# Four value pages per interruption instead of two in the decode attention of a hybrid layer, on one Trainium2 core

## What is computed

```python
xn = rms_norm(x, g_mix)
z = jnp.einsum('btd,dc->btc', xn, w_in)            # q | k | v | forget logits | lru x | lru gate
att = forgetting_attention(q, k_all, v_all, logf_all, n_past)   # 8 heads of 128
lru = jax.nn.gelu(gl) * hs                          # conv, gates, RG-LRU
x = x + jnp.einsum('btc,cd->btd', concat(rms_norm(att), rms_norm(lru)), w_out)
x = x + jnp.einsum('btf,fd->btd', square(relu(rms_norm(x) @ w_up)), w_down)
```

## Time and profile before

| | |
|---|---|
| median of 3 runs | 2301.18 us (2300.08 to 2302.46) |
| span of the profiled execution, first to last instruction | 2298.8 us |
| TensorE busy | 2255.5 us, 98% |
| granted TensorE clock, mean | 0.994 |
| VectorE busy | 1605.5 us, 70% |
| moved | 368.47 MB, mean 160 GB/s |
| step period in the loop | 67.2 us |

### The profile page before, as it was taken

How to read it: one execution, slowest core, us unless ns; L and a number is a source line. 1 busy time by engine, 2 the same in 40 slices (tenths; PEclk the granted TensorE clock), 3 DMA queues, 4 the chain that set the end, 5 groups by cost and what they waited for, 6 DMA issues and landing times.

```text
span 2298.8 us, 50026 instructions
## 1 busy us (share of the span) xinstructions
PE 2255.5 (98%) x19889; PEld 2196.1 (96%) x19889; DVE 1605.5 (70%) x2043; ACT 858.9 (37%) x1201; POOL 154.0 (7%) x194
## 2 busy tenths in 40 slices
PE   7999999999999999999999999999999999999997
PEld 6999898989988999999999999999999999999997
DVE  7349889988884597876576576576576576576563
ACT  5124433344454233343243243243243243243245
POOL 0001111111114031000000000000000000000002
PEclk8999999999999999999999999999999999999998
DMA  7458999999985333333433433433433433433422
GB/s 239 106 159 261 323 330 327 317 314 327 317 290 191 98 127 84 114 96 99 138 93 98 137 93 98 137 93 99 137 94 98 137 93 99 137 93 99 137 89 97
DMA packets 386972, 368.47 MB, mean 160 GB/s; under 512 B 12259, under 2 KB 350596, under 8 KB 385844
## 3 DMA queue, kind: packets, MB, share of 16 engines
q1 hardware_dynamic: 359828, 295.38, 41.9%
q0 software_dynamic: 18608, 67.64, 8.2%
q10 hardware_dynamic: 8448, 4.20, 0.6%
HBM read 354.22 MB, written 12.94 MB: 160 GB/s over the span
## 4 chain that ended last, share of the span: by engine, by line
PE 87%; DVE 6%; DVEq 2%; issue 2%; ACT 1%; DMA 1%; SPq 1%; ACTq 0%
PE PS L1896 37%; PE PS L1900 18%; PE PS L2344 9%; PE PS L2343 9%; PE PS L2342 9%; DVE KR L1349 2%; PE PS L2057 2%; DVEq L1507 1%; PE PS L2105 1%; DVE WL L1213 1%; PE PS L2247 1%; DVE SC L1351 0%; ACT WH L743 0%; PE PS L2095 0%; DVE NM L1506 0%
## 5 line engine op out<-in xcount | busy, mean ns | idle before, releaser
L1093 ACT ACTIVATE WH<-RAW 128x1024 fp32r<-128x1024 f32 x293 | 304.9, 1056 | 679.8 <-PE PS L1900 521.5
L1647 DVE TENSOR_TENSOR WL<-RAW,WH 128x1024 fp32r<-128x1024 f32 x293 | 358.3, 1223 | 133.8 <-ACT WH L1093 132.4
L1896 PE MATMUL PS<-XH,WH 128*128 128x260 f32 x1952 | 408.6, 291 | 10.4 <-DVE XL L1278 6.2
L1896 PE MATMUL PS<-HH,WH 128*128 128x260 f32 x2048 | 412.5, 282 | 1.4 <-DVE HL L1652 0.7
L1900 PE MATMUL PS<-HH,WL 128*128 128x260 f32 x2048 | 411.7, 282 | 0.0
L1896 PE MATMUL PS<-HL,WH 128*128 128x260 f32 x2048 | 410.8, 282 | 0.0
L1896 PE MATMUL PS<-XL,WH 128*128 128x260 f32 x1952 | 393.7, 283 | 0.0
L1900 PE MATMUL PS<-XH,WL 128*128 128x260 f32 x1952 | 393.3, 283 | 0.0
L1750 DVE TENSOR_TENSOR A<-A,PS 128x520 f32<-128x520 f32 x256 | 177.5, 696 | 264.5 <-PE PS L1900 263.8
L1896 PEld LDWEIGHTS PS<-XH,WH 128*128 128x128 f32 x1952 | 301.4, 189 | 28.3 <-issue 19.5
L1896 PEld LDWEIGHTS PS<-HH,WH 128*128 128x128 f32 x2048 | 314.6, 188 | 2.1 <-issue 1.1
(11 more groups left out here) (335 smaller groups left out, 3085.6 us busy)
## 6 DMA issues: line engine op xcount, KB each, us to landing
KR<-in_cache_k POOLq DMA_DIRECT2D x128, 512.0 KB, 6.0
VR<-in_cache_v SPq DMA_DIRECT2D x128, 512.0 KB, 6.3
RAW<-in_w_up SPq DMA_DIRECT2D x128, 512.0 KB, 4.2
RAW<-in_w_down SPq DMA_DIRECT2D x128, 512.0 KB, 4.5
RAW<-in_w_in SPq DMA_DIRECT2D x82, 512.0 KB, 6.6
RAW<-in_w_out SPq DMA_DIRECT2D x32, 512.0 KB, 5.5
TMP<-in_w_up SPq DMA_DIRECT2D x30, 512.0 KB, 6.1
xT_spill<-A SPq DMA_DIRECT2D x1, 4160.0 KB, 16.3
```

The costliest lines, as they stand in the source:

```text
L1093: nc.scalar.activation(RING_H[SLOT[i]], RB[b], ACT.Copy).then_inc(f_hi, 1)
L1647: V.tensor_tensor(RING_L[SLOT[i]], RB[op_block(i)], RING_H[SLOT[i]].bitcast(F32), ALU.subtract).then_inc(f_lo, 1)
L1896: mm(dsts[c], wh(k), x[:, k, c * HT:(c + 1) * HT], start=first and n == 0 and x is xh, stop=False)
```

## The change

`values` takes a third argument, the number of pages. In the steps it is now four (NVS, the ring's size) instead of two, at the places (1, 21), (2, 21), (3, 21) for pages 0 to 3, 4 to 7, 8 to 11, and at (0, 21) of the next step for pages 12 to 15. The places (2, 5), (3, 5), (0, 5) and (1, 3) fall away. The interruption for pages 10 and 11 of sequence 6 in the first output unit falls away too, since step 7 now has them at (3, 21). All later calls keep two pages. SyncE's, GpSimd's, VectorE's and ScalarE's instructions are the same, in the same order.

```diff
-        VALUES_AT = {(1, 21): 0, (2, 5): 2, (2, 21): 4, (3, 5): 6, (3, 21): 8}
-        OLDER_AT = {(0, 5): 10, (0, 21): 12, (1, 3): 14}
+        VALUES_AT = {(1, 21): 0, (2, 21): 4, (3, 21): 8}
+        OLDER_AT = {(0, 21): 12}
...
-            def values(h, b0):
+            def values(h, b0, pages):
...
-                for b in (b0, b0 + 1):
+                for b in range(b0, b0 + pages):
                     pe.wait_ge(v_full[b % NVS], 16 * (NPG // NVS * h + b // NVS + 1))
...
-                        f.append(lambda: values(i - 1, VALUES_AT[q, n]))
+                        f.append(lambda: values(i - 1, VALUES_AT[q, n], NVS))
                     if prev and older and (q, n) in OLDER_AT:
-                        f.append(lambda: values(i - 2, OLDER_AT[q, n]))
+                        f.append(lambda: values(i - 2, OLDER_AT[q, n], NVS))
...
-                if k == NH + 1:
-                    values(last_b - 1, 10)
                 if k == NH + 4:
-                    values(last_b - 1, 12)
+                    values(last_b - 1, 12, 2)
```

More of the change, by code:

```diff
@@ L2273, in head_scores @@
                 value_cols(last_b - 1)
-            out_unit(1, {3: [lambda: values(last_b - 1, 14)], 7: [lambda: max_rows(NB, MT_LAST)], 11: [lambda: max_all(NB, MAX_LAST)],
+            out_unit(1, {3: [lambda: values(last_b - 1, 14, 2)], 7: [lambda: max_rows(NB, MT_LAST)], 11: [lambda: max_all(NB, MAX_LAST)],
                          14: [head_scores]})
[L2277 to L2281, removed]
+            out_unit(2, {7: [lambda: transpose_probs(h)], 13: [lambda: values(last_b, 0, 2)], 19: [lambda: attend(h)],
+                         27: [lambda: values(last_b, 2, 2)]})
+            out_unit(3, {3: [lambda: values(last_b, 4, 2)], 11: [lambda: values(last_b, 6, 2)], 19: [lambda: values(last_b, 8, 2)],
+                         27: [lambda: values(last_b, 10, 2)]})
+            out_unit(4, {3: [lambda: values(last_b, 12, 2)], 11: [lambda: values(last_b, 14, 2)], 17: [last_states], 23: [merge_sums]})
             out_unit(5, {5: [lambda: value_cols(last_b)], 13: [lru_sums]})
```

## The result

The change makes the kernel slower: 2344.41 us (median of 4 runs, 2336.95 to 2346.56) against 2300.63 (4 runs, 2298.89 to 2302.46), a ratio of 1.0184 with the interval [1.0172, 1.0196]. The profiled execution is the fastest of the four, 2336.95 us, with a span of 2335.3; all that follows accounts for its 36.5 us over the span before, and the other three runs are 6 to 10 us longer for a reason that no trace shows. Forecast were 2332 us with the range 2303 to 2348.

What follows compares the result with a forecast made beforehand. A step was taken as VectorE's piece (24.1 us) plus TensorE's piece (the other 43). Path +2.1 and page 11's waits 28.7 gave 30.8 us on the median 2301.2: 2332 us, range 2303 to 2348.

Steps and rivals of the forecast that it cites:

- main term: At (3, 21), page 11 lands later than the 14.9 us after page 8's request allowed; seven waits, 28.7 us.
- 6.5 and 7.1 for sequences 0 and 5: Page 11's forecast lateness at (3, 21), the two longest of seven; the others 2.5 to 3.8 us.
- The landing taken as fixed: Page 11's landing at (3, 21) does not move with earlier requests, which only queue; hence 28.7 us, not 8.
- A: The forecast case: waits for page 11 at (3, 21), full clock, 2325 to 2337 us; chance 0.60.
- C: Rival: earlier requests for pages 10 and 11 help, waits together 8 us, time 2311; chance 0.11.
- can now be requested some 3 us earlier: Pages 10 and 11: slots free after (2, 21), so SyncE need not wait for (3, 5).
- VectorE's piece, gain 0: From `max_all` to normalization, 24.1 us: 1.49 us less TensorE work becomes wait at the transposes, 0.44 to about 1.9.
- The wait for XL behind the gates: After step 7, first output unit: TensorE's 0.93 us wait becomes about 2, so the dropped interruption gains 0.
- The path's own +2.1: TensorE's work without new waits: +0.25 us in each of six passages, +1.5, and +0.56 after step 7.
- The shield at (0, 21): The wait at (3, 21) moves the need for pages 12 to 15 back by as much, so they hold.
- rival B: Clock falls in long waits: two falls of 3.9 us, 2340; in all seven, 2359; chance 0.13.
- the granted clock under 1.00 between 200 and 669 us: Sign of being wrong: this clock reading in the steps would point to B, the clock falling in long waits.

Runs made afterwards that it cites:

- wait-alone kernel: Kernel before, nothing merged; TensorE also waits at (3, 21) until pages 10 and 11 have landed; 2340.12 us, ratio 1.0171.
- experiment 4: The changed kernel, but in unit 3 SyncE requests pages 8 to 11 ahead of the weight unit; 2313.97 us, ratio 1.0052.
- Experiment 6: Kernel before with one pair merged: pages 0 to 3 at (1, 21), (2, 5) gone; 2299.51 us in one run.
- Experiment 5: The changed kernel with all four pages requested ahead of the weights in units 3 and 0, steps 1 to 7; 2304.51 us, ratio 1.0016.
- experiment 3: The changed kernel with 18 unread products added between pages 9 and 10 at (3, 21); 2331.18 us, ratio 1.0127.

## Why the prediction was right, and where not

- **The verdict and its main term.** "Page 11 is the fourth, and too late" was right in each of seven steps and is most of the loss; the sum was 28.7 us forecast, 24.8 measured, and 28.9 as idle time in the wait-alone kernel.
- **Which sequences.** Forecast were 6.5 and 7.1 for sequences 0 and 5; measured were 6.04, 5.87 for 0 and 1, and 3.01 for 5. Step by step the forecast took one trace for a pattern. (Its rows 7 leave out sequences 1 to 3; the trace has them, 18.7, 17.8 and 17.4 us from page 8's request to page 11's landing.) Where the weights stand between the pages, page 11 lands 20 to 22 us after page 8's request in at most two sequences of seven and 16.7 to 19.7 in the rest, and the long ones differ: 0 and 5 before, 0 and 1 after, 3 and 4 in the wait-alone kernel. Whether they move between runs of one kernel no second trace shows. The sum came out near, the single terms did not.
- **The landing taken as fixed** (A against C). It was 17.1 to 20.9 us against 17.4 to 22.0, so this held. The reason given, the full queue, is borne out by experiment 4: with the weights behind them the pages land after 12 to 13. The claim that they "can now be requested some 3 us earlier" was too large: 2.2 for page 10, 0.3 for page 11 in step 5, since the weight request stood before page 10 in SyncE's order and SyncE then stood 3.01 us in the issue itself.
- **VectorE's piece, gain 0.** It is unchanged (24.77 in both), and line 2095 waits 1.74 where about 1.9 was forecast. Experiment 6 shows it by itself. The wait for XL behind the gates was forecast at about 2 and is 2.12.
- **The path's own +2.1.** Experiment 5 has 42.70 against 42.66 forecast. The shield at (0, 21) was right too; it was forgotten in what was expected of experiment 4.
- **The step that failed: the clock.** The forecast's case kept full clock, and the rival B had two falls of 3.9 us. Measured: a fall in all seven steps at 1.5 us each, 10.6 in all, and from the transposes of one step to those of the next 71.4 to 71.7 us in steps 3 to 6, where a step of 70.5 was forecast. So the granted clock under 1.00 between 200 and 669 us, which the forecast itself named as a sign of being wrong, did come, and 2344.4 lies above the 2325 to 2337 of its case A. Both halves of B's working were wrong: that waits of 3 us speak against a fall (waits of 2.06 us had one), and the price, which came from a 13.7 us stretch while the stretches here are 3.4 or 6.8 us long, partly idle. By the page "TensorE: Matmul & The Clock Gate" of the Trainium skill (section "Why this matters for your kernels") the clock falls when TensorE idles too long between bursts. The trace agrees in kind, 2.06 us idle and then 3.4 us at 0.50, but not in the length: here the clock fell behind waits shorter than that section names, and did not fall behind one of 2.75 us in the wait-alone kernel.
- **Right by offset.** 28.7 was 3.9 too much and the clock's 10.6 was missing; with the 0.84 earlier start the profiled span comes out 5.7 us over the sum. So the total came near partly by luck. The median is 12.4 over the forecast: these 5.7, and the 7.5 by which the profiled run lies under the median of the runs, less 0.8, since the forecast added 2.4 us around the span where this run has 1.6. The 7.5 stay open. More sequences with a long landing would do it, as the spread above allows, but no trace shows such a run.

## What to carry to other kernels

Ask of each interruption in which piece of the path it lies: one that lies where the engine waits anyway can be fed with work, and merging there saves nothing. A ring whose slots are all wanted in one place has no prefetch left, so the time from the first slot's request to the last slot's landing, read under the real queue, must be under the spacing of the places; if it isn't, put the small urgent requests ahead of the bulk ones. And count a short wait on TensorE at more than its length where the clock is seen to fall behind it.

## What the runs showed of the hardware

- Short waits were enough for the granted clock to fall to 0.50, and their length alone does not decide it. It fell with all seven waits at (3, 21) in the change (2.06 us in three steps, in step 7 only 0.49 and 1.35, close together), with one of 1.99 in the wait-alone kernel, and with the four of 2.11 to 2.13 for XL in the output units. It did not fall with one of 2.75 in step 7 of the wait-alone kernel, one of 2.12 behind the added products of experiment 3, nor with any of 1.73 to 1.74 at the transposes. Of seven kernels with a wait of 1.83 to 1.86 in step 1, three had a fall there. Between 200 and 760 us the low stretches last 3.4 or 6.8 us; one at (3, 21) cost 1.5 us, while the one at 716.2 in the output units cost nothing that can be seen.
- Issuing page 10, with pages and weights outstanding, held SyncE for 2.3 to 3.5 us in steps 1 to 6 of the change and 0.8 to 2.2 before it, where 0.33 is usual. With unit 3's pages first (experiment 4) none of its four took longer than 0.33 in step 5, but the issues of pages 12 and 14 behind them took 1.8 and 2.8.
- The same four requests of 512 KB have landed 12 to 13 us after the first (experiment 4), or 17 to 22 (before and after the change), by whether a weight unit of 1 MB stands between them in the same queue.
- With useless products to do in the wait the kernel was faster than with TensorE left idle, 2331.18 us against 2344.41, since in steps 2 to 6 the clock held.
